# Output projections by token halves, with each half's norm and FFN operand blocks made apart

## The chip, the cores and the metric

The program runs on one core of one Trainium2 chip. The time is that of one execution on the device, in microseconds; the median of a few runs is given, and one more execution was profiled. In the profile PE is TensorE's matmuls, PEld its weight loads, DVE is VectorE, ACT ScalarE, POOL GpSimd, SP the sync engine that issues most DMAs. L12 is line 12 of the kernel.

## What is computed

A trunk of two layers over x of 1024 tokens by 1024 features, in float32. Layer 0 mixes tokens by sliding-window attention, layer 1 by "forgetting" attention; behind each follow the output projection with a residual, a norm, and a SwiGLU FFN with 2816 hidden features.

```python
for i in range(DEPTH):
    h = _rmsnorm(x, norm_mix[i])
    ...
        mix = _swa_sink_mixer(h, swa_w_in[j], swa_sinks[j], swa_w_out[j], cos, sin)
    ...
        mix = _fox_mixer(h, fox_w_in[j], fox_f_bias[j], fox_w_out[j])
    x = x + mix.astype(x.dtype)
    h = _rmsnorm(x, norm_ffn[i])
    x = x + _swiglu(h, ffn_w_gate_up[i], ffn_w_down[i]).astype(x.dtype)
return _rmsnorm(x, norm_final)
```

## The kernel before

**Form.** Everything is kept transposed: features on the 128 partitions, tokens along the row. x is `x_t`, 8 feature tiles (KD = 8) of 1024 tokens; "half" 0 and 1 are tokens 0 to 511 and 512 to 1023. A float32 product is made of three matmuls on parts: each operand has a high part (ScalarE, a copy into fp32r) and a low part (VectorE, raw minus high), and high x high, high x low and low x high are summed in PSUM. So each weight strip is loaded (SP), gets `w_hi` (ScalarE, `high`) and `w_lo` (VectorE, `low`), and is then used by TensorE. There are two buffers of each; semaphore `w_split` counts finished low parts, `mm_done` finished half strips, `evac_done` evacuated ones.

**Order.** Each engine's program is written out by hand, and the engines meet by semaphores. There is no scheduler; an engine does its own list in order, and a wait holds up all that stands behind it.

**Output projection** (`out_projection` on PE, `update_out` on ACT and DVE). A strip is 128 output features; strip m is done over half 0 and half 1 (24 matmuls of 512 tokens each) into bank 0 or 1, resp. 2 or 3. `out_first` does most of strip 0 while the attention is ending. VectorE adds each half strip to x (`add_strip`), ScalarE squares it and stores the strip of x to DRAM, GpSimd adds the squares up in `ssq`. While the last strips run, the first FFN weight tile is split (`weight_high`, `weight_low`).

**Head of the FFN** (`ffn`, `norm_sums`, `norm_bc`, `blocks_dve`, `block_high`). TensorE sums `ssq` over the partitions into bank 5 (L1703), ScalarE takes the root, VectorE makes the factor by six short steps and a diagonal (L1203 to L1214), TensorE spreads it over the partitions (L1710), ScalarE copies it to `rstd_ffn`. VectorE then makes normed blocks of x: `n00`, `n10` (half 0), `n01`, `n11` (half 1), 4 feature tiles each, and three more from their differences; seven blocks `b`, each with a high and a low part. The FFN's first product is done by Strassen's scheme in the form of Winograd: seven products (NP = 7, 12 matmuls each) per hidden tile instead of eight. There are 22 hidden tiles (FT) in a layer; tile r has gate and up weights `a_raw`, sums of these (`weight_sums` on GpSimd), and seven split blocks `a`. Products 4 to 6 wait for copies that ScalarE and VectorE take out of PSUM (`p1_keep`, `p5_keep`, `p57_keep`). The products of tile 0 and 1 stand one behind the other.

**Down projection.** The hidden tiles go through DRAM (`hid_scr`) and come back in three groups of 8, 6 and 8 tiles (`set_full`), are split into `set_hi` and `set_lo`, and every group is run over 8 strips. The first four tiles of group 0 come back early into `hid_pre`. TensorE begins groups 1 and 2 when all `set_lo` of the group are there.

**Entry of layer 1.** `update_ffn` adds the last strips; ScalarE makes `h_hi` from them, and VectorE makes the 16 half pieces of `h_lo` when all strips are done.

## Time and profile before

| | us |
|---|---|
| median of 3 runs | 2517.53 |
| lowest and highest run | 2513.55, 2517.95 |
| the profiled execution | 2513.21 |
| its span, from the first to the last instruction | 2511.1 |
| TensorE busy (share of the span) | 2340.7 (93%) |
| VectorE busy | 1369.9 (55%) |
| ScalarE busy | 971.9 (39%) |
| GpSimd busy | 592.3 (24%) |

The mean granted clock of TensorE was 0.967 of full speed. The page's slices show it below full speed at the start and at two places, about 450 to 500 us and 1750 to 1850 us from the start; there also the busy share of TensorE falls. In these places the output projection of a layer has ended and its FFN begins. Matmuls overlap in the records (one of 512 columns is shown with 390 ns and follows the one before by 227 ns at full clock), so their starts are to be read rather than their sums.

### The profile page before, as it was taken

The page shows a single profiled execution, that of the slowest core. Times are in us where ns is not written, and L with a number is a line of the kernel's source. Part 1 is how long each engine was busy: PE and PEld are TensorE (multiplying, and loading weights), DVE is VectorE, ACT ScalarE, POOL GpSimd, SP SyncE. Part 2 cuts the span into 40 slices and gives each one's busy share as a digit, 9 for nine tenths or more (in the row PEclk, how much of TensorE's full clock was granted, in tenths as well). Part 3 has the DMA queues.
Part 4 walks back from the last instruction along what each step waited for, and adds up shares of the span by engine and source line. Part 5 has one row for each costly group of instructions (what it writes and reads, how often), then busy time and mean ns, then how long its engine had stood idle before and what let it go on. Part 6 is the DMA issues. An engine that isn't in the chain of part 4 may idle for free.

```text
span 2511.1 us, 33488 instructions
## 1 busy us (share of the span) xinstructions
PE 2340.7 (93%) x11188; PEld 1931.9 (77%) x11188; DVE 1369.9 (55%) x2174; ACT 971.9 (39%) x1866; POOL 592.3 (24%) x423
## 2 busy tenths in 40 slices
PE   4998999699999999999999989989699999999998
PEld 3776777488888887786888778878478888888777
DVE  7797952844445443324633489982664444453422
ACT  3116942433333421232212289982343333331223
POOL 3232423133233100020000056652222322300011
PEclk6999999799999999999999999999799999999999
DMA  5258433022322262222444587745122222252311
GB/s 188 84 174 202 94 118 117 25 76 81 94 75 75 100 226 67 84 101 68 141 136 151 177 192 167 167 112 173 42 72 79 75 86 90 75 205 84 118 46 75
DMA packets 289811, 283.38 MB, mean 113 GB/s; under 512 B 64704, under 2 KB 253504, under 8 KB 285008
## 3 DMA queue, kind: packets, MB, share of 16 engines
q1 hardware_dynamic: 269536, 225.60, 31.7%
q10 hardware_dynamic: 20208, 56.92, 6.1%
q8 instruction: 37, 0.61, 0.1%
q14 instruction: 30, 0.25, 0.0%
HBM read 200.63 MB, written 81.85 MB: 112 GB/s over the span
## 4 chain that ended last, share of the span: by engine, by line
PE 78%; DVE 14%; ACT 3%; issue 2%; POOL 1%; ACTq 1%; DMA 0%; SPq 0%; DVEq 0%; POOLq 0%
PE psum L1688 12%; PE psum L1690 12%; PE psum L1689 12%; PE psum L1920 11%; PE psum L1922 11%; PE psum L1924 11%; PE psum L1814 2%; DVE work_b L1579 2%; PE psum L1832 2%; PE psum L1833 1%; DVE b_lo L1405 1%; PE psum L1781 1%; PE psum L1782 1%; DVE swa_p_lo L1297 1%; DVE neg_max L1261 1%
## 5 line engine op out<-in xcount | busy, mean ns | idle before, releaser
L1920 PE MATMUL psum<-b_hi,a_hi 128*128 128x512 f32 x1232 | 484.7, 393 | 38.6 <-DVE b_lo L1405 33.6
L1922 PE MATMUL psum<-b_lo,a_hi 128*128 128x512 f32 x1232 | 483.5, 392 | 0.0
L1924 PE MATMUL psum<-b_hi,a_lo 128*128 128x512 f32 x1232 | 483.2, 392 | 0.0
L1920 PEld LDWEIGHTS psum<-b_hi,a_hi 128*128 128x128 f32 x1232 | 233.9, 190 | 92.6 <-issue 38.0
L1688 PE MATMUL psum<-set_hi,dw_hi 128*128 128x512 f32 x704 | 277.2, 394 | 16.0 <-DVE set_lo L1443 16.0
L1360 DVE TENSOR_TENSOR x_t<-psum,x_t 128x512 f32<-128x512 f32 (+1 forms) x128 | 88.4, 692 | 371.8 <-PE psum L1690 357.0
L1689 PE MATMUL psum<-set_lo,dw_hi 128*128 128x512 f32 x704 | 276.6, 393 | 0.0
L1690 PE MATMUL psum<-set_hi,dw_lo 128*128 128x512 f32 x704 | 276.4, 393 | 0.0
L1924 PEld LDWEIGHTS psum<-b_hi,a_lo 128*128 128x128 f32 x1232 | 233.9, 190 | 49.1
L1922 PEld LDWEIGHTS psum<-b_lo,a_hi 128*128 128x128 f32 x1232 | 234.0, 190 | 48.6
L1688 PE MATMUL psum<-h_hi,w_hi 128*128 128x512 f32 x576 | 230.3, 400 | 19.6 <-DVE w_lo L1184 14.3
L693 POOL TENSOR_TENSOR score<-score,inv_l 128x128 f32<-128x128 f32 (+7 forms) x128 | 155.4, 1225 | 383.1 <-DVE inv_l L1278 383.0
L727 POOL TENSOR_TENSOR a_sum<-a_raw 128x512 f32<-128x512 f32 x88 | 116.0, 1319 | 487.9 <-DVE a_lo L1400 487.4
L1689 PE MATMUL psum<-h_lo,w_hi 128*128 128x512 f32 x576 | 227.4, 395 | 0.0
L1690 PE MATMUL psum<-h_hi,w_lo 128*128 128x512 f32 x576 | 227.1, 394 | 0.0
L1400 DVE TENSOR_TENSOR a_lo<-a_sum,a_hi 128x512 fp32r<-128x512 f32 x176 | 125.9, 718 | 102.4 <-ACT a_hi L976 102.1
L1688 PEld LDWEIGHTS psum<-set_hi,dw_hi 128*128 128x128 f32 x704 | 133.6, 190 | 47.3 <-issue 16.3
L976 ACT ACTIVATE a_hi<-a_sum 128x512 fp32r<-128x512 f32 x176 | 109.7, 628 | 132.3 <-PE psum L1924 132.3
L1689 PEld LDWEIGHTS psum<-set_lo,dw_hi 128*128 128x128 f32 x704 | 133.7, 190 | 28.1
L1690 PEld LDWEIGHTS psum<-set_hi,dw_lo 128*128 128x128 f32 x704 | 133.7, 190 | 27.8
L795 ACT ACTIVATE dw_hi<-dw_raw 128x1024 fp32r<-128x1024 f32 x48 | 50.7, 1055 | 255.1 <-PE psum L1690 255.1
L1688 PEld LDWEIGHTS psum<-h_hi,w_hi 128*128 128x128 f32 x576 | 110.4, 192 | 46.0 <-issue 16.2
(193 smaller groups left out, 4269.6 us busy)
## 6 DMA issues: line engine op xcount, KB each, us to landing
a_raw<-in_ffn_w_gate_up SPq DMA_DIRECT2D x88, 512.0 KB, 5.0
hid_scr<-hid_out SPq DMA_DIRECT2D x44, 512.0 KB, 5.8
set_full<-hid_scr SPq DMA_DIRECT2D x18, 1024.0 KB, 6.1
x_t<-x_scr SPq DMA_DIRECT2D x16, 1024.0 KB, 7.4
dw_raw<-in_ffn_w_down SPq DMA_DIRECT2D x32, 512.0 KB, 4.1
x_scr<-x_t ACTq DMA_DIRECT2D x24, 512.0 KB, 2.7
w_raw<-in_fox_w_in SPq DMA_DIRECT2D x24, 512.0 KB, 4.0
fox_qk_hi<-part_hi ACTq DMA_DIRECT2D x16, 512.0 KB, 2.6
```

Source lines behind the costliest of these rows:

```text
L693: last = nc.gpsimd.tensor_tensor(sc, sc, inv_l[sl][:, i:i + 1].to_broadcast([P, fox_w(t)]), ALU.mult)
L727: nc.gpsimd.tensor_tensor(a_sum[dst][:, :, :], in0, in1, op).then_inc(a_summed, 1)
L795: nc.scalar.activation(dw_hi[p][:, :, :], dw_raw[p][:, :, :], ACT.Copy).then_inc(w_high, 1)
L976: nc.scalar.activation(a_hi[i][:, :, :], a_block(q, i), ACT.Copy).then_inc(a_high, 1)
L1360: V.tensor_tensor(xs, bank[2 * p + h].unsqueeze(1), xs, ALU.add).then_inc(evac_done, 1)
L1400: V.tensor_tensor(a_lo[i][:, :, :], a_block(q, i), a_hi[i][:, :, :].bitcast(FP32), ALU.subtract)\
L1688: T.matmul(bank[2 * p + h], whi[:, k, :], mh[:, k, half(h)], start=k == 0, stop=False)
L1689: T.matmul(bank[2 * p + h], whi[:, k, :], ml[:, k, half(h)], start=False, stop=False)
L1690: last = T.matmul(bank[2 * p + h], wlo[:, k, :], mh[:, k, half(h)], start=False, stop=k == n - 1)
L1920: T.matmul(out_ps, a_hi[i][:, j, :], b_hi[i][:, j, :], start=not more and j == 0, stop=False, skip_group_check=True)
L1922: T.matmul(out_ps, a_hi[i][:, j, :], b_lo[i][:, j, :], start=False, stop=False, skip_group_check=True)
L1924: last = T.matmul(out_ps, a_lo[i][:, j, :], b_hi[i][:, j, :], start=False, stop=j == KH - 1, skip_group_check=True)
```

## The change

1. **The output projection goes by token halves.** It now has 16 steps j = 0 to 15 per layer: strips 0 to 7 over half 0, then strips 0 to 7 over half 1, each 24 matmuls into bank j mod 4. Every strip of weights is loaded and split for each half. `o_hi` and `o_lo` are two tiles each, one per half.
2. **Norm and blocks of half 0 are made during half 1.** After step 9 the sums of half 0 are taken, after step 10 the factor is spread, and `n00`, `n10` and the parts of blocks 0 and 1 are made in steps 11 to 14. The square of strip 7 isn't added up by GpSimd but summed by TensorE directly, so there are two short matmuls for each of four token tiles.
3. **The splits of the first FFN weight tile** are spread over steps 2 to 8; its loads and those of tile 1 come ahead of the strip loads of step 4 and later.
4. **Look-ahead products.** Product 0 of tile 0 comes before the sums of half 1, product 1 of tile 0 behind them, then the factor is spread, then come products 0 and 1 of tile 1, then 2 to 6 of each. `prod_mm` is split into `prod_a` (products 0, 1) and `prod_b`.
5. **Down projection.** `hid_pre` is gone. Group 0 is taken in the order 6, 7, 0 to 5, tiles 6 and 7 being loaded after product 1 of the last tile, the others after product 3. In groups 1 and 2 `set_hi` and `set_lo` stand ahead of the weight split and the addition of the same strip.
6. **Entry of layer 1.** The pieces of `h_lo` are made strip by strip, and the first two weight strips of layer 1 go into the buffers of the down projection.
7. **A new memory map.** Nearly all tiles have other addresses, and there is a third buffer for the keys in layer 0. Other than above, no order or wait changes in attention, input projections and the FFN loop.

The core of the diff:

```diff
+        K_ORDER = (6, 7, 0, 1, 2, 3, 4, 5)
...
+            def load_out(c0, view, layer):
+                for j in range(2, 4):
+                    load_out_w(c0, view, j)
+
+                sp.wait_ge(mm_done, 2 * (c0 + 1))
+                load_a(layer, 0, 0)
+                load_a(layer, 1, 1)
+                for j in range(4, 2 * KD):
+                    load_out_w(c0, view, j)
...
-                sp.dma_start(hid_pre[:, :, :], hid_scr[:, 0:4, :]).then_inc(pre_in, 16)
...
+                sp.wait_ge(prod_a, 2 * (last + 1))
...
+                load_set(0, 3, 0)
+                load_d(c0, 0, 0, n0)
+                sp.wait_ge(prod_b, 5 * last + 2)
+                load_set(0, 0, 0)
+                load_set(0, 1, 0)
+                load_set(0, 2, 0)
...
+                    act.wait_ge(*prod_at(r, 5))
+                    set0_high(layer, (2, 3, 4, 5))
...
                 for m in range(KD):
-                    d_high(c0 + m + 2, m % 2)
                     if m >= 2:
                         if m % 2 == 0:
-                            act.wait_ge(set_in[1 + m // 2], 16 * (2 * layer + 1))
+                            act.wait_ge(set_in[m // 2 - 1], 16 * (2 * layer + 1))
                         set_high_of(set_hi[1][:, m - 2, :], set_full[1][:, m - 2, :])
+                    d_high(c0 + m + 2, m % 2)
...
+            def update_out(c0, layer, back, k):
+                for j in range(2 * KD):
+                    h, m = j // KD, j % KD
+                    if j == 0:
+                        dve.wait_ge(x_back[back], 16)
+                    if j == 2:
+                        dve.wait_ge(x_back[back + 1], 48)
+                    dve.wait_ge(mm_done, 2 * (c0 + j) + 2)
+                    V.tensor_tensor(x_t[:, m, half(h)], bank[j % 4], x_t[:, m, half(h)], ALU.add).then_inc(evac_done, 2)
+                    if j < 2 * KD - 2:
+                        low(c0 + j + 2, j % 2)
+                    if 0 <= j - 2 < NP:
+                        weight_low(FT * layer, 0, j - 2)
+                    if j == KD + 2:
+                        norm_diag(k, 0)
+                    if j == KD + 3:
+                        dve.wait_ge(rstd_ready, 2 * k + 1)
+                        normed(layer, k, n00, 0, 0)
+                    if j == KD + 4:
+                        normed(layer, k, n10, 1, 0)
+                    if j == KD + 5:
+                        block_low(layer, 0, n00)
+                    if j == KD + 6:
+                        block_low(layer, 1, n10)
...
+            def out_projection(a, c0, k, layer):
+
+                pe.wait_ge(w_split, c0 + 2)
                 out_first(a, 1, range(early_tiles(a)), True)
 
                 pe.wait_ge(a.o_free, a.groups * a.units)
-                for h in range(2):
-                    out_first(a, h, range(early_tiles(a), KD), False).then_inc(mm_done, 1)
-                chunk(c0 + 1, 1, KD, o_hi, o_lo)
-                linear_rest(c0, KD // 2, KD, o_hi, o_lo)
...
+                for m in range(2):
+                    out_first(a, m, range(early_tiles(a), KD), False).then_inc(mm_done, 2)
+                for j in range(2, 2 * KD):
+                    h, p = j // KD, j % 2
+                    pe.wait_ge(w_split, c0 + j + 1)
+                    if j >= 4:
+                        pe.wait_ge(evac_done, 2 * (c0 + j - 3))
...
+                    last.then_inc(mm_done, 2)
+                    if j == KD + 1:
+                        norm_sums(k, 0)
+                    if j == KD + 2:
+                        norm_bc(k, 0)
...
             def ffn(layer, c0, k):
-                norm_sums(k)
-                norm_bc(k)
-                r0 = FT * layer
-                products(r0, 0, NP * layer)
-                products(r0 + 1, 1)
+                r0, b0 = FT * layer, NP * layer
+                pe.wait_ge(evac_done, 2 * (c0 - 1))
+                product(r0, 0, 0, b0)
+                norm_sums(k, 1)
+                product(r0, 0, 1, b0)
+                norm_bc(k, 1)
+                for i in range(2):
+                    product(r0 + 1, 1, i)
+                for i in range(2, NP):
+                    product(r0, 0, i, b0)
+                for i in range(2, NP):
+                    product(r0 + 1, 1, i)
```

**The order at three places.** A row is an instruction with output, inputs and what it waits for; a number behind a name tells buffers apart, and x2 is a repeat. First, PE where the early part of the output projection of layer 0 ends, before and after:

```order
L1848 MATMUL psum<-o_hi_93,w_hi0_121 128x512
L1849 MATMUL psum<-o_lo_94,w_hi0_121 128x512
L1850 MATMUL psum<-o_hi_93,w_lo0_123 128x512
L1688 MATMUL psum<-o_hi_93,w_hi1_122 128x512 [waits evac_done,w_split]
```

```order
L1905 MATMUL psum<-o_hi0_95,w_hi1_126 128x512
L1906 MATMUL psum<-o_lo0_97,w_hi1_126 128x512
L1907 MATMUL psum<-o_hi0_95,w_lo1_128 128x512
L1964 MATMUL psum<-o_hi0_95,w_hi0_125 128x512 [waits w_split]
```

Before, the second strip (buffer 1) follows on the first; now both have been done for half 0, and the third strip, in buffer 0 again, follows.

Second, DVE in layer 0 from the projection's end to the first normed block before, and around the factor of half 0 (step 10) after:

```order
L1360 TENSOR_TENSOR x_t_49<-psum,x_t_49 128x512 [waits mm_done] x2
L1203 TENSOR_SCALAR nat_v_212<-psum 128x8 [waits sd_done]
...
L1214 TENSOR_TENSOR diag_ffn_166<-ident_204,nat_y_213 128x1024 [waits newton]
L1414 SCALAR_TENSOR_TENSOR n00_189<-x_t_49,gains_209,rstd_ffn_167 128x512 [waits rstd_ready]
L1414 SCALAR_TENSOR_TENSOR n00_189<-x_t_49,gains_209,rstd_ffn_167 128x512 x3
```

```order
L1415 TENSOR_TENSOR x_t_49<-psum,x_t_49 128x512 [waits mm_done]
L1226 TENSOR_TENSOR w_lo0_127<-w_raw0_123,w_hi0_125 128x1024 [waits w_high]
L1247 TENSOR_SCALAR nat_v_217<-psum 128x4 [waits sd_done]
...
L1259 TENSOR_TENSOR diag_ffn_173<-ident_209,nat_y_218 128x512 [waits newton]
L1415 TENSOR_TENSOR x_t_49<-psum,x_t_49 128x512 [waits mm_done]
L1226 TENSOR_TENSOR w_lo1_128<-w_raw1_124,w_hi1_126 128x1024 [waits w_high]
L1463 SCALAR_TENSOR_TENSOR n00_194<-x_t_49,gains_214,rstd_ffn_174 128x512 [waits rstd_ready]
L1463 SCALAR_TENSOR_TENSOR n00_194<-x_t_49,gains_214,rstd_ffn_174 128x512 x3
```

The factor now stands behind the addition and the weight split of step 10, and the first normed block behind those of step 11.

Third, DVE at the last strip of group 1 of the down projection (`dw_lo` is the low part of a weight strip), before and after:

```order
L1360 TENSOR_TENSOR x_t_49<-psum,x_t_49 128x512 [waits mm_done] x2
L1190 TENSOR_TENSOR dw_lo1_197<-dw_raw1_193,dw_hi1_195 128x1024 [waits w_high]
L1443 TENSOR_TENSOR set_lo0_200<-set_full0_202,set_hi0_198 128x1024 [waits set_high]
```

```order
L1491 TENSOR_TENSOR set_lo0_205<-set_full0_207,set_hi0_203 128x1024 [waits set_high]
L1405 TENSOR_TENSOR x_t_49<-psum,x_t_49 128x512 [waits mm_done] x2
L1232 TENSOR_TENSOR dw_lo1_202<-dw_raw1_198,dw_hi1_200 128x1024 [waits w_high]
```

The set's low part stood last in the strip and now stands first.

## Rows read from the trace of the kernel before

**Rows 1.** Waits of PE over the span: us in total, times, longest.
```profile
PE psum L1920 <- DVE b_lo L1405: 33.6, 4, 8.6
PE psum L1688 <- DVE set_lo L1443: 16.0, 8, 3.7
PE psum L1688 <- DVE h_lo L1392: 5.3, 1, 5.3
```

**Rows 2.** Timeline of PE, head of layer 0: start, us, instruction, [idle before <-releaser].
```profile
435.62 3.09 PE L1703 MATMUL psum<-ones,ssq 128*128 128x1 f32 x16 [2.87 <-POOL ssq L747]
...
442.55 3.78 PE L1710 MATMUL psum<-diag_ffn,ones 128*128 128x512 f32 x4 [3.85 <-DVE diag_ffn L1214]
454.74 0.76 PE L1920 MATMUL psum<-b_hi,a_hi 128*128 128x512 f32 x1 [8.40 <-DVE b_lo L1405]
...
471.17 0.76 PE L1920 MATMUL psum<-b_hi,a_hi 128*128 128x512 f32 x1 [8.22 <-DVE b_lo L1405]
...
484.53 0.47 PE L1920 MATMUL psum<-b_hi,a_hi 128*128 128x512 f32 x1 [2.13 <-ACT p_keep L1014]
```

**Rows 3.** Stretches: us; busy PE, PEld, DVE, ACT, POOL; PEclk, DMA share, GB/s.
```profile
432.60:509.10 76.50, 51.03 (x189) 39.50 (x189) 58.06 (x60) 30.82 (x36) 16.86 (x13) 0.80 0.10 32
1778.50:1857.00 78.50, 52.00 (x189) 40.15 (x189) 58.03 (x60) 30.92 (x36) 16.85 (x13) 0.76 0.10 31
471.20:476.70 5.50, 5.50 (x13) 4.33 (x14) 5.50 (x3) 4.41 (x3) 0.00 (x0) 0.50 0.00 0
982.00:986.00 4.00, 3.97 (x11) 3.13 (x12) 0.00 (x0) 0.00 (x0) 0.00 (x0) 0.57 1.10 346
1147.10:1153.10 6.00, 5.99 (x14) 4.72 (x15) 6.00 (x10) 0.00 (x0) 0.00 (x0) 0.51 0.32 87
```

**Rows 4.** Timeline of DVE, steady projection of layer 0.
```profile
389.38 0.69 DVE L1360 TENSOR_TENSOR x_t<-psum,x_t 128x512 f32 x1 [4.73 <-PE psum L1690]
391.93 1.42 DVE L1184 TENSOR_TENSOR w_lo<-w_raw,w_hi 128x1024 fp32r<-128x1024 f32 x1 [1.86 <-ACT w_hi L789]
394.82 0.69 DVE L1360 TENSOR_TENSOR x_t<-psum,x_t 128x512 f32 x1 [1.47 <-PE psum L1690]
```

**Rows 5.** Timeline of PE, first matmul of group 1, down projection of layer 0.
```profile
982.03 0.52 PE L1688 MATMUL psum<-set_hi,dw_hi 128*128 128x512 f32 x1 [3.69 <-DVE set_lo L1443]
```

**Rows 6.** Timeline of DVE, the last set_lo before it.
```profile
980.67 1.22 DVE L1443 TENSOR_TENSOR set_lo<-set_full,set_hi 128x1024 fp32r<-128x1024 f32 x1
```

**Rows 7.** Timeline of DVE, head of layer 0: diagonal, two normed blocks, low part of block 0.
```profile
441.27 1.23 DVE L1214 TENSOR_TENSOR diag_ffn<-ident,nat_y 128x1024 f32<-128x1024 f32 x1
447.00 5.39 DVE L1414 SCALAR_TENSOR_TENSOR n<-x_t,gains,rstd_ffn 128x512 f32<-128x512 f32 x8 [4.50 <-ACT rstd_ffn L807]
452.31 2.28 DVE L1405 TENSOR_TENSOR b_lo<-n,b_hi 128x2048 fp32r<-128x2048 f32 x1
```

**Rows 8.** Timeline of DVE, last weight split before layer 1's first matmul.
```profile
1144.86 1.45 DVE L1184 TENSOR_TENSOR w_lo<-w_raw,w_hi 128x1024 fp32r<-128x1024 f32 x1 [2.31 <-ACT w_hi L789]
```

**Rows 9.** A stretch at the end of the FFN products of layer 0, as rows 3.
```profile
884.00:890.00 6.00, 6.00 (x28) 4.95 (x28) 3.76 (x6) 3.40 (x5) 0.00 (x0) 1.00 1.01 390
```

**Rows 10.** Timeline of PE, first matmul of the second strip, layer 0.
```profile
356.43 0.39 PE L1688 MATMUL psum<-o_hi,w_hi 128*128 128x512 f32 x1
```

**Rows 11.** Timeline of ACT, high part of the third strip, layer 0.
```profile
361.90 1.06 ACT L789 ACTIVATE w_hi<-w_raw 128x1024 fp32r<-128x1024 f32 x1 [3.85 <-DMA w_raw<-in_swa_w_out]
```

**Rows 12.** Timeline of DVE, low part of the third strip, layer 0.
```profile
362.99 1.23 DVE L1184 TENSOR_TENSOR w_lo<-w_raw,w_hi 128x1024 fp32r<-128x1024 f32 x1 [5.67 <-ACT w_hi L789]
```

**Rows 13.** Timeline of ACT, head of layer 0: three high parts of blocks in a row.
```profile
468.86 5.51 ACT L990 ACTIVATE b_hi<-b_full 128x2048 fp32r<-128x2048 f32 x3 [5.26 <-DVE b_full L1420]
```

**Rows 14.** DMA issues: KB each, median us from issue to landing.
```profile
w_raw<-in_swa_w_out SPq DMA_DIRECT2D x8, 512.0 KB, 5.1
```

**Rows 15.** Timeline of POOL in the same stretch.
```profile
390.97 1.29 POOL L747 TENSOR_TENSOR ssq<-ssq,sq 128x512 f32<-128x512 f32 x1 [4.07 <-ACT sq L924]
```

**Rows 16.** Tile set_full, 850 to 960 us.
```profile
DMA to landing us min/median/max: 5.1/6.2/11.3
```

More of the change, by code:

```diff
@@ L992, in set_high_of, with set0_high, products_act @@
             def set_high_of(dst, src):
                 nc.scalar.activation(dst, src, ACT.Copy).then_inc(set_high, 1)
-            def products_act(r, q, last=False, layer=0, c0=0):
+            def set0_high(layer, ks):
+                for k in ks:
+                    if k % 2 == 0:
+                        act.wait_ge(set0_in[k // 2], 16 * (layer + 1))
+                    set_high_of(set_hi[0][:, k, :], set_full[0][:, k, :])
+            def products_act(r, q, first=False, last=False, layer=0, c0=0):
@@ L997, in products_act @@
                 bk = lambda i: prod_bank(q, i)
-                act.wait_ge(prod_mm, NP * r + 1)
+                act.wait_ge(*prod_at(r, 0))
                 wait(act, c_done, 4 * r - 3)
                 nc.scalar.activation(p1_keep[:, :], bk(0), ACT.Copy).then_inc(p1_kept, 1)
-                if not last:
+                if not last and not first:
                     weight_high(r + 1, 1 - q, 0)
                     weight_high(r + 1, 1 - q, 1)
-                else:
-                    act.wait_ge(pre_in, 16 * (layer + 1))
-                    for k in range(4):
-                        set_high_of(set_hi[0][:, k, :], hid_pre[:, k, :])
@@ L1443, in set_low_of, with set0_low, products_dve @@
                 V.tensor_tensor(dst, src, high_part.bitcast(FP32), ALU.subtract).then_inc(set_low, 1)
-            def products_dve(r, j, q, last=False, layer=0, c0=0):
+            def set0_low(layer, at0, ks):
+                for n, k in enumerate(ks):
+                    dve.wait_ge(set_high, FT * layer + at0 + n + 1)
+                    set_low_of(set_lo[0][:, k, :], set_full[0][:, k, :], set_hi[0][:, k, :])
+            def products_dve(r, j, q, first=False, last=False, layer=0, c0=0):
                 bk = lambda i: prod_bank(q, i)
@@ L1490, in products_dve @@
                 if last:
-                    for k in range(4, 6):
-                        dve.wait_ge(set_high, FT * layer + k + 1)
-                        set_low_of(set_lo[0][:, k, :], set_full[0][:, k, :], set_hi[0][:, k, :])
-                dve.wait_ge(prod_mm, NP * r + 7)
+                    set0_low(layer, 4, (2, 3, 4, 5))
+                dve.wait_ge(*prod_at(r, 6))
                 V.tensor_tensor(hid_h[0], bk(6), u2_keep[:, :], ALU.add).then_inc(c_done, 1)
@@ L1675, in _, with chunk @@
             T = nc.tensor
-            def chunk(c, p, n, mh, ml, ready=None, after=None, w=(w_hi, w_lo)):
+            def chunk(c, p, n, mh, ml, ready=None, after=None, w=(w_hi, w_lo), order=None):
                 whi, wlo = w[0][p], w[1][p]
@@ new lines, in product @@
+            def product(r, q, i, blocks=None):
+                pe.wait_ge(a_low, NP * r + i + 1)
+                if blocks is not None:
+                    pe.wait_ge(b_low, blocks + i + 1)
+                if i == 4:
+                    pe.wait_ge(p1_kept, r + 1)
+                if i == 5:
+                    pe.wait_ge(p5_kept, r + 1)
+                if i == 6:
+                    pe.wait_ge(p57_kept, r + 1)
+                out_ps, more = prod_bank(q, i), i >= 4
+                for j in range(KH):
+                    T.matmul(out_ps, a_hi[i][:, j, :], b_hi[i][:, j, :], start=not more and j == 0, stop=False,
+                             skip_group_check=True)
+                    T.matmul(out_ps, a_hi[i][:, j, :], b_lo[i][:, j, :], start=False, stop=False,
+                             skip_group_check=True)
+                    last = T.matmul(out_ps, a_lo[i][:, j, :], b_hi[i][:, j, :], start=False, stop=j == KH - 1,
+                                    skip_group_check=True)
+                last.then_inc(prod_at(r, i)[0], 1)
@@ L1986, in _ @@
             attention(fox)
[L1987 removed]
+            out_projection(fox, C_O1, 3, 1)
             ffn(1, C_F1, 3)
```

598 lines of the change are left out of this document (292 added, 306 removed).

## The prediction

> **What bounds the kernel now.** I read the waits of TensorE first, then its timeline around the longest of them, then the other engines' timelines at those places. TensorE is busy nearly throughout, so its waits are the time to be won. Three belong to what the change touches: on b_lo, the low parts of the activation blocks (33.6 us, four waits), on set_lo (16.0 us, eight waits) and on h_lo (5.3 us, one) [rows 1]. The b_lo waits stand in one place in each layer, which I call the head: from the last matmul of the output projection to the end of the first two tiles of FFN products. In layer 0 TensorE waits there 2.87, 3.85, 8.40, 8.22 and 2.13 us, and has 3.09 us of column sums and 3.78 us of spreading matmuls between [rows 2]. The head takes 76.5 us in layer 0 and 78.5 in layer 1, at a granted clock of 0.80 and 0.76 [rows 3]. VectorE adds into x one half strip of 24 matmuls every 5.44 us in the steady projection (389.38 to 394.82) [rows 4], so a product of 12 takes 2.72 us and the 14 products of the head 38.1. The heads therefore lose 38.4 and 40.4 us, **78.8 us** together; with the set and h waits that is all the change can touch.
>
> **Price of a low clock.** After the 8.22 us wait the granted clock is 0.50 for 5.5 us: 2.7 us lost. After a 3.69 us wait it is 0.57 for 4 us: 1.7 us; the other three of this kind I read the same way, a little less, 6.1 us for all four. After the h_lo wait it is 0.51 for 6 us: 2.9 us [rows 3].
>
> **Part 1, group changes of the down projection: a gain of 20.9 us.** Four times TensorE waits 3.69 us at the start of a group, for the last set_lo, which VectorE does behind the last strip's addition and the next weight split [rows 5, 6]. The change puts set_hi and set_lo ahead of these, so the last set_lo is made while the last strip (8.2 or 10.9 us of matmuls) still runs: its set_hi comes behind the weight split of two strips ahead, about 2.2 us into that strip, and set_lo is done by 3.5 us. VectorE's addition now stands behind set_lo; who waits for it is the bank's next use, a whole strip later. 4 x 3.69 + 6.1 = 20.9. What then is late is nothing on TensorE.
>
> **Part 2, into layer 1: a gain of 6.5 us.** The 16 h_lo pieces (0.67 us each, the rate of [rows 7]) are made strip by strip, and only those of the last two strips are left at the end. From the end of the last strip: addition 0.8, h_hi and square 1.2, weight high part 1.05, weight low part 1.45 [rows 8], two pieces 1.35 and one 0.67, that is 6.5 us, where TensorE reaches the last piece after 21 matmuls, 4.8 us. A wait of 1.7 us stands for 5.3 + 2.9.
>
> **Part 3, end of the FFN products: a loss of 3.8 us.** The early 2 MB load of hid tiles 0 to 3 is gone. Instead tiles 6 and 7 come after the second product of the last tile and 3 MB after the fourth. DMA moved 390 GB/s in the like stretch of before [rows 9], so 3 MB are in about 9.5 us after issue, while 8.2 us of products remain. That alone would be covered, since the tiles come one by one. But set_hi of tiles 2 to 5 now writes over a block that product six reads. After that product come an addition (0.7) that stands behind two set_lo, a Silu (0.6), then set_hi and four set_lo at 1.2 us. By my schedule the last is ready 7.2 us after the last product, TensorE wants it after 4.8 (21 matmuls): 2.5 us lost. Before lost (16.0 - 14.8) / 2 = 0.6. So 1.9 more in each layer.
>
> **Part 4, the head and the projection before it: a loss of 8.0 us.** The same matmuls, but what TensorE loses changes place. I list what it loses in a layer, in order.
> (a) Third strip. TensorE used to do strip 2 over both halves (10.9 us) after the early strip; strip 2 is now done for one half, ahead. It arrives where it used to start strip 2, at 356.43 [rows 10], and needs strip 3, whose raw weights land behind 4 MB of x: high part at 361.90, low part from 362.99 for 1.23 us [rows 11, 12]. The order of the loads hasn't changed. Wait 7.8 us, clock 2.7.
> (b) The sums for the first half: 3.1, eight pairs of short matmuls as before, now twice in a layer.
> (c) Spreading of the first half. TensorE reaches it right after strip 11 of 16; VectorE starts the factor only behind the addition and weight split of that same strip. Addition to end of split 3.95 us (389.38 to 391.93, plus 1.42) [rows 4], factor and half a diagonal 2.1 (the row's 1.23 us is a whole one [rows 7]; the step in which GpSimd isn't in the way is short). Wait 6.0, matmul 1.0, clock 2.7: 9.7.
> (d) Strips 12 to 16. VectorE has per half strip 3.95 us of chain in 5.44; with four normalising instructions more (2.7; eight take 5.39 [rows 7]) it has 6.7 us and falls behind by 1.3 and 2.6 us, then has a block's low part (2.28) too. Only strip 16 comes late, by 0.9.
> (e) Second sums 3.1. The square they need is ready under the first look-ahead product.
> (f) Second spreading: from the sums' end to it 3.84 us before [rows 2], less half a diagonal 0.6, under a product of 2.72: wait 0.5, matmul 1.0.
> (g) Block 3 (n01, a difference, n11, its low part): copy 0.7 + 2.7 + 2.2 + 2.7 + 2.3 = 10.6 us, under two look-ahead products, 5.4: wait 5.2, clock 2.7.
> (h) Block 4: two differences and a low part, 6.6 us against a product with low clock, 5.4: wait 1.4 with the signal.
> (i) Block 5. ScalarE's last three high parts took 5.51 us in a row [rows 13], 1.84 each; two of them now wait for the last difference, and p1_keep comes behind: 2.2 + 3.7 + 0.6 against 2.7: wait 3.8, clock 1.5. p5_keep then is just in time.
> Sum 10.5 + 3.1 + 9.7 + 0.9 + 3.1 + 1.5 + 7.9 + 1.4 + 5.3 = 43.4 us a layer, 86.8 for both against 78.8. The work of VectorE that went under the projection (two blocks, seven splits of a) is real, about 14 us a layer; (a), (c) and the second sums take it back.
>
> **Supply.** Each strip is loaded and split twice, 0.5 MB every 5.44 us in place of 10.9. A load is issued when the split of two strips before is done and has 8.3 us; it took 5.1 [rows 14]. Two 1 MB loads of a go ahead of strip 5 now; the 7.8 us wait covers them. GpSimd does its four a_sum ahead of the squares' sums, also under that wait. At nothing, then; bounds 0 and the rival below.
>
> The split took 1.42 us with a GpSimd addition (1.29) beside it, 1.23 without [rows 4, 12, 15]: 0.2 us, under cover in my sum. The Trainium skill (SBUF — State Buffer, "SBUF: two separate sides") says that such a VectorE instruction and GpSimd's take a shared port pair as a lock, and the loser waits for the whole of the other. By it strips 13 to 15, where VectorE is behind already, could each lose up to 1.29 us, and (d) would grow by some 2 us: 2506 in place of 2502. The row, of an instruction that came late into the addition, doesn't contradict it.
>
> **Sum.** -20.9 - 6.5 + 3.8 + 8.0 = -15.6 us. The profiled execution took 2513.2 (span 2511.1), so 2497.6; it lies 4.3 under the median of the three runs, 2517.5, against which I forecast **2502**.
>
> **Rivals.** First, *the heads gain after all*: strip 3 lands 1 us earlier, as no x store runs beside it, the short steps of the factors take no contention (1.5 in all) and the clock costs half (4.8). That is 7.3 us a layer: 2487. For it, the clock fell back for one stretch only after 3.69 us; against it, (a), (c) and (g) are over 5 us each, like the waits that cost 2.7.
> Second, *no change*: VectorE is the bound of the whole second half. It misses each strip from 13 on and the differences slip; some 7 us a layer more, 2516. For it, (d) has no slack at all; against it, chain (c) is measured with its neighbours.
> Third, *slower, by weight supply*: if a strip's load takes L us, each of six pairs of strips in two layers waits L - 8.3. The loads of 1 MB landed in 5.1 to 11.3 us [rows 16]; at 11.3 it is 12 x 3.0 = 36, 2538. It decides from 10.1 us on (12 x 1.8 = 21). Against it, 5.1 us with half the traffic.
>
> **How the numbers follow.** The forecast, 2494 to 2510, has 0.52, the gaining heads 0.17, no change 0.19, slower 0.12. For 8 in 10 the range goes from 2485, half of the first rival, to 2518, where the second ends. 0.2% is 5 us, about what a measurement can tell: faster is below 2512.5, all of the first two and a quarter of the third, 0.74; same 0.14; slower 0.12.
>
> **What the profile after would show.** Right: no wait on set_lo of 3.7 us; a wait of about 8 us for w_lo at the third strip of both projections and of 6 before the first spreading matmul; the b_lo waits down from 33.6 to about 14; a wait near 2 us at the entry of layer 1. Wrong: a wait for a weight split at every strip (third rival), or third strip and first spreading without a wait, when the sum would be 25 us or more better.

## The result and the profile after

| | before | after |
|---|---|---|
| median of 4 runs each, on one chip, us | 2516.30 | 2490.56 |
| lowest and highest | 2513.55, 2517.95 | 2488.18, 2493.86 |
| span of the profiled execution, us | 2511.1 | 2490.1 |
| mean granted clock of it | 0.967 | 0.976 |

The ratio is 0.9903 (95% interval 0.9891 to 0.9914): **faster by 25.7 us**, 21.0 between the two profiled executions. The forecast was 2502 us, 15.6 below.

Those waits of TensorE in the kernel after that answer to [rows 1] or are new (us in total, times, longest):

```profile
PE psum L1986 <- DVE b_lo L1457: 20.1, 6, 5.4
...
PE psum L1964 <- DVE w_lo L1226: 14.4, 5, 7.9
PE psum L1768 <- DVE diag_ffn L1259: 11.5, 2, 5.8
...
PE psum L1738 <- DVE set_lo L1491: 3.1, 8, 1.1
...
PE psum L1738 <- DVE h_lo L1437: 1.5, 2, 1.2
```

The wait on set_lo fell from 16.0 to 3.1 us and the one on h_lo from 5.3 to 1.5. The waits on b_lo fell from 33.6 to 20.1, but the line on w_lo, of the output projection, is new, and the line on diag_ffn grew from 7.6 (3.85 of it in [rows 2]) to 11.5. So in the output projection and the head the waits changed place more than they went away. For b_lo the forecast was about 14: the 7.0 us above it are twice the wait of 3.50 us, which the prediction had given to a copy, and run 7 shows that the copy ended it.

TensorE's timeline of the same kernel through layer 0, in order of time, answers to [rows 2, 5, 10]:

```profile
365.63 0.79 PE L1964 MATMUL psum<-o_hi,w_hi 128*128 128x512 f32 x1 [7.88 <-DVE w_lo L1226]
...
424.85 1.22 PE L1768 MATMUL psum<-diag_ffn,ones 128*128 128x512 f32 x1 [5.75 <-DVE diag_ffn L1259]
...
451.09 0.50 PE L1964 MATMUL psum<-o_hi,w_hi 128*128 128x512 f32 x1 [0.39 <-DVE w_lo L1226]
...
476.10 0.77 PE L1986 MATMUL psum<-b_hi,a_hi 128*128 128x512 f32 x1 [5.38 <-DVE b_lo L1457]
...
482.71 0.47 PE L1986 MATMUL psum<-b_hi,a_hi 128*128 128x512 f32 x1 [1.15 <-DVE b_lo L1457]
...
489.20 0.76 PE L1986 MATMUL psum<-b_hi,a_hi 128*128 128x512 f32 x1 [3.50 <-DVE b_lo L1457]
...
897.28 0.50 PE L1738 MATMUL psum<-set_hi,dw_hi 128*128 128x512 f32 x1 [0.98 <-DVE set_lo L1491]
...
983.10 0.39 PE L1738 MATMUL psum<-set_hi,dw_hi 128*128 128x512 f32 x1
```

The first six are items (a), (c), (d), (g), (h), (i) of the prediction's fourth part. The last is the first matmul of group 1: where [rows 5] shows a wait of 3.69 us there is none.

To see where 21.0 us went I cut both spans at the same matmuls (columns: us between the two cuts):

| stretch | before | after | change |
|---|---|---|---|
| attention, up to where TensorE turns to the second (after: third) strip | 356.43 | 357.75 | +1.3 |
| layer 0: rest of projection and head, to the end of the first two tiles' products | 152.71 | 154.87 | +2.2 |
| end of the FFN products to group 1's first matmul | 92.09 | 89.68 | -2.4 |
| group 1, group 2 | 159.63 | 152.33 | -7.3 |
| entry of layer 1 and fox attention | 560.68 | 557.29 | -3.4 |
| layer 1: projection and head | 154.69 | 153.22 | -1.5 |
| layer 1: as lines 3 and 4 | | | -9.6 |
| end | 21.54 | 21.24 | -0.3 |

The FFN loops between the cuts take 380.80 us in both. The two down projections are the only large item.

### The profile page after: what moved, and what is told of

Its sections match the earlier page's. It is cut to its first block, busy times and chain, and to the rows that moved or that the text cites. A ratio compares the mean times of both kernels' runs of the same rounds, so it can differ in the third digit from the quotient of the medians.

```text
span 2490.1 us, 33386 instructions
## 1 busy us (share of the span) xinstructions
PE 2339.4 (94%) x11220; PEld 1930.0 (78%) x11220; DVE 1398.7 (56%) x2204; ACT 987.2 (40%) x1884; POOL 589.5 (24%) x419
## 4 chain that ended last, share of the span: by engine, by line
PE 77%; DVE 14%; ACT 4%; issue 2%; DMA 2%; POOL 1%; ACTq 1%; SPq 0%; DVEq 0%
PE psum L1986 11%; PE psum L1988 11%; PE psum L1990 11%; PE psum L1738 10%; PE psum L1739 10%; PE psum L1740 10%; PE psum L1872 2%; DVE work_b L1629 2%; PE psum L1964 2%; PE psum L1890 2%; PE psum L1965 2%; PE psum L1966 2%; PE psum L1891 1%; PE psum L1839 1%; PE psum L1840 1%
## 5 line engine op out<-in xcount | busy, mean ns | idle before, releaser
L1986 PE MATMUL psum<-b_hi,a_hi 128*128 128x512 f32 x1232 | 484.8, 393 | 20.1 <-DVE b_lo L1457 20.1
L1738 PE MATMUL psum<-h_hi,w_hi 128*128 128x512 f32 x544 | 216.1, 397 | 14.5 <-DVE w_lo L1226 14.5
L1740 PE MATMUL psum<-h_hi,w_lo 128*128 128x512 f32 x544 | 213.7, 393 | 0.0
L1739 PE MATMUL psum<-h_lo,w_hi 128*128 128x512 f32 x544 | 213.7, 393 | 0.0
L1405 DVE TENSOR_TENSOR x_t<-psum,x_t 128x512 f32<-128x512 f32 x96 | 66.1, 690 | 237.1 <-PE psum L1740 226.3
L824 ACT ACTIVATE w_hi<-w_raw 128x1024 fp32r<-128x1024 f32 x66 | 69.3, 1050 | 170.5 <-PE psum L1740 162.8
```

Of the source, the lines that this page charges most:

```text
L824: nc.scalar.activation(w_hi[p][:, :, :], w_raw[p][:, :, :], ACT.Copy).then_inc(w_high, 1)
L1405: V.tensor_tensor(xs, bank[2 * p + h].unsqueeze(1), xs, ALU.add).then_inc(evac_done, 1)
L1738: T.matmul(bank[2 * p + h], whi[:, k, :], mh[:, k, half(h)], start=i == 0, stop=False)
L1739: T.matmul(bank[2 * p + h], whi[:, k, :], ml[:, k, half(h)], start=False, stop=False)
L1740: last = T.matmul(bank[2 * p + h], wlo[:, k, :], mh[:, k, half(h)], start=False, stop=i == n - 1)
L1986: T.matmul(out_ps, a_hi[i][:, j, :], b_hi[i][:, j, :], start=not more and j == 0, stop=False, skip_group_check=True)
```

## Experiments

Times are medians. The kernels of this section ran in three groups, each on one chip beside runs of the kernel before: 1 to 3 and 5 (before 2516.0 us), 4, 6, 7 and the first of 8 (2514.2), the rest (2515.8). The kernel before thus differs by up to 2 us between groups; where that matters, the ratio to it is used as well. The traces are cut as in the table above, and "head" means the rest of the projection and the head. Numbers of runs below are those of the headings.

### 1 and 2. The group order alone, and everything but it

The edit of the first, in the kernel before; the second is its reverse in the kernel after.

```diff
                     for m in range(KD):
-                        add_strip(c0 + KD * gi + m, m, m % 2)
-                        d_low(c0 + KD * gi + m + 2, m % 2)
...
                             set_low_of(set_lo[1 - gi][at0], set_full[1 - gi][at0], set_hi[1 - gi][at0])
+                        add_strip(c0 + KD * gi + m, m, m % 2)
+                        d_low(c0 + KD * gi + m + 2, m % 2)
```

ScalarE's `d_high` goes behind `set_high_of` in the same way.

> The kernel before, with one part of the change alone: in each output group of the FFN's down projection the products of a set stand ahead of the ones whose operand pieces are made late, in the order of the kernel after. Nothing else differs. Theory (the group order brings nearly all of the gain): minus 20 to 24 us, so about 2494 us; in the trace the two groups of a layer lose the waits on set_lo that they had (group 1 of layer 0 ends about 5.5 us sooner after its start, its start about 4 us sooner), and the heads are as before. Rival (the output projection by halves and the block entry bring the gain, the groups only fill other waits): minus 0 to 8 us, about 2512 us.

> The kernel after with that one part undone: the groups in the order of the kernel before, all else as after. Theory: plus 20 to 24 us over the kernel after, so about 2513 us, close to the kernel before, because the rest of the change nets only minus 2 to minus 4 us (the entry of layer 1 minus 4.7, the heads plus 0.7, the end of the FFN's products has its price of 3.0 from h_lo). Rival: the rest of the change holds its own gain of 10 us or more, and this kernel stays under 2505 us.

Measured: 2490.6 us for the groups alone, 25.3 below the kernel before and a little more than the 20 to 24 expected (ratio to before 0.9902, 0.9887 to 0.9917), 2511.5 for the rest alone (0.9984, 0.9974 to 0.9993). The wait on set_lo in the groups-alone kernel, and VectorE's last set_lo of group 1, which stood right ahead of the waiting matmul in [rows 6]:

```profile
PE psum L1688 <- DVE set_lo L1443: 1.2, 4, 0.5
```

```profile
970.43 1.23 DVE L1190 TENSOR_TENSOR dw_lo<-dw_raw,dw_hi 128x1024 fp32r<-128x1024 f32 x1 [0.46 <-ACT dw_hi L795]
971.58 1.22 DVE L1443 TENSOR_TENSOR set_lo<-set_full,set_hi 128x1024 fp32r<-128x1024 f32 x1
974.72 0.69 DVE L1360 TENSOR_TENSOR x_t<-psum,x_t 128x512 f32<-128x512 f32 x1 [1.93 <-PE psum L1690]
```

It ends at 972.8; group 1 begins at 979.96. The addition, now behind it, waits for TensorE and not the other way round. From the first matmul of group 0 to the last of group 2 it is 240.34 us where before took 251.5, in each layer: 22.3 us in all. **The group order brings all of the gain, and the other three parts together bring nothing beside it that these runs can tell from none.** With the old groups they gained 4.5 us, a little more than the 2 to 4 us expected of them, so the pair was run once more on one chip.

> The kernel before with the group order alone, once more, beside the kernel after on one chip, to tell whether the rest of the change (output projection by halves, h_lo with the strips, memory map) moves the time at all where the groups are in order. By the landmarks of the two first traces the rest costs 1.3 us; by the run of the kernel after with the old groups it gains 4.5 us; by the single run of the groups alone it is nothing. Theory: within 2 us of the kernel after. Rival (the rest gains, as in the run with the old groups): 3 to 6 us above the kernel after.

> The kernel after as it is, on the same chip as the groups alone. Theory: 2490 us, within 2 us of the groups alone. Rival: 3 to 6 us below them.

Measured: 2491.3 and 2489.8 us, 1.5 apart, as the theory had it and in either's spread (2489.7 to 2492.7 and 2487.8 to 2491.1). Cut by cut between these two traces, the rest of the change costs 3.7 us up to the end of layer 0's head and 1.5 at the end of the FFN's products of each layer, and gets 8.3 back from the end of layer 0's down projection to the end of layer 1's head.

### 3. The third strip's weight

```diff
             def load_out(c0, view, layer):
-                for j in range(2, 4):
-                    load_out_w(c0, view, j)
...
                 k = 2 if a.fox else 0
+                for j in range(2, 4):
+                    load_out_w(C_O1 if a.fox else C_O0, w_out_view["fox" if a.fox else "swa"], j)
                 sp.wait_ge(a.pv_done, a.groups * a.units - 1)
```

> The kernel after; the loads of strips 2 and 3 of the output weight are issued on SyncE's queue ahead of the load of x, whose issue waits for the attention products to be done. Theory (the third strip's products wait for their weight because its load is queued behind that issue): the wait of 7.9 us on w_lo in layer 0 falls to about 2.7 us and that of 5.6 us in layer 1 to about 3.3 us, and with the lower clock behind them gone the kernel gains 8 to 11 us, about 2481 us. Rival (VectorE's own work, the splits and the sums of squares that stand ahead, sets the wait): the wait stays above 6 us and 4.5 us and the time moves by less than 2 us.

Measured: 2484.6 us (0.9880, 0.9865 to 0.9895), 6 us below the kernel after: less than expected. In layer 1 the third strip's wait went from 5.55 to 3.07 and the head took 148.7 us in place of 153.2. In layer 0 TensorE now has two waits. The first is at the third strip, the second two strips later, at strip 4 counted from 0, the fifth; the expectations call it the fourth:

```profile
358.41 0.50 PE L1963 MATMUL psum<-o_hi,w_hi 128*128 128x512 f32 x1 [2.39 <-DVE w_lo L1225]
...
375.06 0.50 PE L1963 MATMUL psum<-o_hi,w_hi 128*128 128x512 f32 x1 [3.84 <-DVE w_lo L1225]
```

Following w_lo back, over ScalarE to GpSimd, in the same kernel:

```profile
371.20 0.63 ACT L970 ACTIVATE sq_ffn<-x_t 128x512 f32<-128x512 f32 x1 [10.63 <-POOL ssq_ffn L767]
371.73 1.04 ACT L823 ACTIVATE w_hi<-w_raw 128x1024 fp32r<-128x1024 f32 x1
```

```profile
365.16 2.66 POOL L749 TENSOR_TENSOR a_sum<-a_raw 128x512 f32<-128x512 f32 x2 [24.68 <-DMA a_raw<-in_ffn_w_gate_up]
```

ScalarE stood 10.63 us at a square whose buffer GpSimd had not read, and GpSimd stood behind its a_sum, which wait for a_raw.

### 4. That chain, and ScalarE's order

On top of 3 (`sum_squares_out` now calls `weight_sums` itself, behind its step 1; the same in layer 1):

```diff
-            weight_sums(0, 0)
-            sum_squares_out(0)
+            sum_squares_out(0, 0)
...
                     h, m = j // KD, j % KD
+                    if j < 2:
+                        high(c0 + j + 2, j % 2)
                     act.wait_ge(evac_done, 2 * (c0 + j) + 2)
```

> The kernel with early loads of strips 2 and 3 (it gained only 5.9 us, since a new wait of 3.84 us stood at the fourth strip of layer 0), and two orders more: GpSimd makes the a_sum pieces, which wait for a_raw, behind its second sum of squares and not ahead of the first; ScalarE makes w_hi of strips 2 and 3 ahead of the squares of x of strips 0 and 1. Theory (the fourth strip waited on w_lo, that on w_hi, that on a square that waited for GpSimd, and GpSimd stood in order behind the load of a_raw): the 3.84 us go to under 0.5, the third strip's wait falls from 2.4 and 3.1 us to under 1.5 us, and the kernel comes to 2474 to 2479 us. Rival (the fourth strip's weight is late by its load): 3 us or more stay at the fourth strip of layer 0, and the time stays above 2481 us.

Measured: 2478.7 us (0.9864, 0.9849 to 0.9880), 6 us below run 3, within the theory's number. But at strip 4 of layer 0 (the expectation's fourth) **the rival was right**: 4.35 us of wait are there still, and now it is the load:

```profile
371.50 0.50 PE L1965 MATMUL psum<-o_hi,w_hi 128*128 128x512 f32 x1 [4.35 <-DVE w_lo L1227]
```

```profile
368.86 1.06 ACT L823 ACTIVATE w_hi<-w_raw 128x1024 fp32r<-128x1024 f32 x1 [5.65 <-DMA w_raw<-in_swa_w_out]
```

That strip's load is issued behind four a_raw loads of 0.5 MB. GpSimd was only the later of two causes. The third strips now wait 1.11 and 1.79 us (under 1.5 was expected of both), and the two heads are 3.0 and 3.2 us shorter than in run 3.

### 5. The first half's spreading, one step later

```diff
-                    if j == KD + 2:
+                    if j == KD + 3:
                         norm_bc(k, 0)
```

and the same for ScalarE's copy of it.

> The kernel after; the spreading of the first half's norm over the partitions (the products of diag_ffn with ones, and the copy of them) is moved one step later in the loop of the second half, behind the next strip's products. Theory (TensorE stands in order behind a product whose operand VectorE makes late, while the next strip's products are ready): the waits of 5.75 us on diag_ffn, which cost 9.9 and 9.0 us with their clock, shrink to under 1.5 us each, and the kernel gains 14 to 18 us, about 2475 us. Rival (the next strip's weight is no sooner there than diag_ffn, or the first look-ahead products then wait for the copy): the wait moves to w_lo or to b_hi and b_lo, and the gain is under 5 us.

Measured: 2473.4 us (0.9837, 0.9824 to 0.9850), 17.1 below the kernel after; the two heads are 8.0 and 8.3 us shorter. TensorE's timeline at the spreading:

```profile
423.66 0.70 PE L1768 MATMUL psum<-diag_ffn,ones 128*128 128x512 f32 x1 [0.34 <-DVE diag_ffn L1259]
```

The clock, by stretches of 4 us behind that place (columns as in [rows 3]), first of the kernel after, then of this one:

```profile
424.80:428.80 4.00, 3.95 (x7) 2.49 (x8) 0.00 (x0) 0.60 (x1) 0.00 (x0) 0.50 0.31 93
```

```profile
423.60:427.60 4.00, 3.94 (x15) 2.93 (x16) 2.35 (x3) 2.06 (x3) 1.30 (x1) 1.00 0.68 237
```

5.75 us of wait gave 0.50 (the lower level, 1.2 GHz) behind it, 0.34 us gave 1.00. So item (c), 9.9 us in the kernel after and 9.7 in the prediction, was nearly all wait and low clock (the spreading itself stays), and it is a matter of one step in TensorE's order: the product was asked for one strip before VectorE could have made its operand.

### 6. h_lo at the end again

```diff
-                    if c_next and m:
-                        low_part(m - 1)
                 if c_next:
-                    low_part(KD - 1)
+                    for m in range(KD):
+                        low_part(m)
```

> The kernel after, with one part undone: VectorE makes all eight pieces of h_lo after the last strip of layer 0's FFN, as in the kernel before, instead of one with each strip. Theory (this part brings the gain of layer 1's entry, 4.7 us between the two traces): TensorE's wait on h_lo goes from 1.2 back to about 5.3 us, with a low clock behind it, and the kernel is 4 to 7 us slower than the kernel after, about 2496 us. Rival (the pieces beside the strips cost VectorE as much on the strips as they save at the end): within 1.5 us of the kernel after.

Measured: 2494.4 us (0.9925, 0.9911 to 0.9938), above the kernel after by 3.8 us of medians or, with each beside its own kernel before, by 5.5; the theory had 4 to 7. The wait is 5.30 us again, and from the end of group 2 to TensorE's second strip of layer 1 it takes 17.0 us where the kernel after took 9.4. So the part is worth some 4 to 8 us, which the output projection, the heads and the end of the products give back.

### 7. The copy to p1_keep

```diff
                 norm_spread(k, 1)
+                keep_first(r0, 0)
                 for i in range(2, NP):
                     block_high(layer, i)
```

> The kernel after; ScalarE copies product 0's bank to p1_keep (for block 0 of the first FFN strip pair) before it makes b_hi of blocks 2 to 6, not behind all five. The wait in question is the third one in the FFN's first products, 3.50 us in each layer, which the trace puts down to VectorE's b_lo; product 4 also waits for that copy, which in the kernel after starts at 488.48, behind two b_hi of 3.71 us. Theory (the copy, not b_lo, ends the wait): the wait falls to 1.2 to 1.6 us, and with its clock the kernel gains 4 to 7 us over the two layers, about 2485 us. Rival (b_lo of block 4 ends it, as the trace says): the wait stays at 3.5 us and the time within 1.5 us of the kernel after.

(`keep_first` is the copy to p1_keep. Product 4, counted from 0, is the prediction's block 5.) Measured: 2491.1 us (0.9911, 0.9897 to 0.9924): no change, although the wait behaved as in the theory. TensorE at products 4 and 5:

```profile
484.84 0.47 PE L1991 MATMUL psum<-b_hi,a_hi 128*128 128x512 f32 x1 [1.35 <-issue]
...
491.03 0.47 PE L1991 MATMUL psum<-b_hi,a_hi 128*128 128x512 f32 x1 [3.21 <-ACT p_keep L1055]
```

The theory was right on what ended the 3.50 us: with only the copy moved, it fell to 1.35, although the trace named b_lo. And the gain was nil, since product 5 waits for the next copy, p5_keep. On ScalarE that stands behind the same b_hi and a Silu, and the Silu itself waits 2.13 us for an addition that VectorE makes behind all its low parts. The prediction had called p5_keep "just in time"; it was so only because block 5 was late.

### 8. All of them, and the waits that came next

> All of the orders together: the kernel after with the first half's norm spread one step later, early loads of strips 2 and 3, the two orders of GpSimd and ScalarE, and the early copy to p1_keep. Theory (the waits are apart in time, so their prices add): minus 17 (late spread) minus 14 (loads and orders) minus 5 (copy) from 2490.6, so 2450 to 2459 us. Rival (each wait that goes uncovers the next, most of all that of the first products on b_lo, 5.4 us, whose operands VectorE makes no sooner): less than two thirds of that sum, above 2466 us.

Measured: 2463.8 us (0.9804, 0.9791 to 0.9818), between theory and rival. The parts had by themselves -17.1, -11.9 and +0.5, together -28.5; measured -26.8. So they add; what was too high were the sizes expected of the loads with their orders (14, measured 11.9) and of the copy (5, measured nothing).

> The kernel with all orders (2463.8 us), and three steps more, each against the wait that came in the place of one taken away: ScalarE also copies product 2's bank to p5_keep ahead of b_hi of blocks 5 and 6 (the wait on p_keep of 3.2 us in each layer), VectorE makes p57_keep ahead of the first a_lo piece there, and the load of strip 4's weight is issued ahead of the second a_raw (the wait of 2.1 us at the fourth strip of layer 0). Theory (each of these waits stands behind a step that is only in the wrong place in its engine's order): both waits on p_keep fall under 1 us and the fourth strip's under 0.5 us, 8 to 11 us with their clock, so 2453 to 2456 us. Rival (VectorE is the limit there, whatever the order): the waits move to b_lo or p57_keep of block 6 at over 2 us in each layer, and the time stays above 2460 us.

```diff
+                load_out_w(c0, view, 4)
                 load_a(layer, 1, 1)
...
                 for i in range(2, NP):
+                    if i == 5:
+                        keep_third(r0, 0)
                     block_high(layer, i)
```

(`keep_third` is the copy to p5_keep), and VectorE's p57_keep one a_lo piece sooner. Measured: **2450.1 us (0.9744, 0.9731 to 0.9757)**, 13.7 below the one before it by medians. The forecast was 2453 to 2456, a gain of 8 to 11. By the profiled spans it is 7.4 (2459.6 and 2452.2), the one before being its fastest execution and this one its slowest; the two heads are 5.8 and 3.1 us shorter, 8.9 in all. So the theory's size fits, and no trace shows where the rest of the 13.7 lies. TensorE at strip 4, at blocks 3, 4 and 5, and at the next tile's block 6 (product 5 counted from 0):

```profile
369.21 0.50 PE L1979 MATMUL psum<-o_hi,w_hi 128*128 128x512 f32 x1 [0.80 <-DVE w_lo L1239]
...
457.20 0.77 PE L2001 MATMUL psum<-b_hi,a_hi 128*128 128x512 f32 x1 [5.39 <-DVE b_lo L1470]
...
463.80 0.47 PE L2001 MATMUL psum<-b_hi,a_hi 128*128 128x512 f32 x1 [1.36 <-DVE b_lo L1470]
468.16 0.47 PE L2001 MATMUL psum<-b_hi,a_hi 128*128 128x512 f32 x1 [1.38 <-issue]
...
486.39 0.47 PE L2001 MATMUL psum<-b_hi,a_hi 128*128 128x512 f32 x1 [1.46 <-ACT p_keep L1046]
```

The waits went less far than forecast. Strip 4's went from 2.13 to 0.80 us, not under 0.5. The first tile no longer waits for p5_keep in either layer, but the next tile now does, for 1.46 and 1.41 us.

This kernel beats both: 65.7 us below the kernel before, measured beside it, and some 40 below the one after, with the same matmuls. What stays of the head is block 3's 5.39 us in each layer, which is VectorE's chain of four pieces n01, a difference, four pieces n11 and a low part; that was not attacked.

## Why the prediction came out as it did

The sign held, and so did the mechanism of each part: the group order pays, and the rest, forecast at +5.3 us, comes to about nothing. The median of 2490.6 lies in the wide range (2485 to 2518) but below the narrow one (2494 to 2510). By the cuts of the profiled pair, forecast -15.6, measured -21.0. The medians are 25.7 apart; the other 4.7 us are no term of the sum but the place of the two profiled executions among the others of their kernels, which spread over 4.4 and 5.7 us.

**Part 1, groups.** Forecast -20.9, measured -22.3 (table above and run 1). The waits of 3.69 us are gone, and the clock behind them was worth a little more than read.

**Part 2, entry.** Forecast -6.5, measured -4.7. The wait came out right (forecast 1.7; 1.16 and 0.36 us). The 2.9 us of low clock were taken as gone altogether. In this trace they were not: the stretch of the kernel after behind the two waits, columns as in [rows 3],

```profile
1142.70:1151.60 8.90, 8.90 (x42) 7.57 (x41) 2.33 (x8) 0.27 (x1) 0.00 (x0) 0.81 0.44 117
```

has a clock of 0.81, where 7 matmuls follow each other by 0.43 us, not 0.23, right behind the 16 short ones of the norm's sums. That gives 1.4 back. But it is one execution's number: in the second trace of the same kernel (the last of runs 1 and 2), behind the same two waits and the same short matmuls, the clock stayed at 1.00. Of the nine traces with this entry three show the low clock and six do not.

**Part 3, end of the products.** Forecast +3.8, measured +3.0. TensorE waits four times on set_lo, 0.98 us (1.10 in layer 1) and three times 0.17, which with the slower first matmul behind each wait costs 2.6 us, where I had 2.5. But what the kernel before lost there was 1.2 us in a layer, not 0.6.

**Part 4, heads.** Forecast +8.0, measured +0.7. This is the term that was off. Loss of TensorE in a layer, us, by item:

| item | forecast | layer 0 | layer 1 |
|---|---|---|---|
| (a) third strip | 10.5 | 10.4 | 8.5 |
| (b) first sums | 3.1 | 1.85 | 1.85 |
| (c) first spreading | 9.7 | 9.9 | 9.0 |
| (d) strip 16 | 0.9 | 0.7 | 0.7 |
| (e) second sums | 3.1 | 1.85 | 1.7 |
| (f) second spreading | 1.5 | 1.1 | 1.1 |
| (g), (h), (i) blocks 3 to 5 | 14.6 | 14.8 | 15.1 |
| sum of items | 43.4 | 40.6 | 37.9 |

(Against the ideal 114.24 us of that stretch the losses are 40.6 and 39.0; 1.1 us of layer 1 has no item.) **The mis-sized step is (b) and (e)**: I took the 3.09 us of [rows 2] for 16 short matmuls over as they stood. But those ran behind a wait of 2.87 us, at a low clock. The stretch of before, and that of after:

```profile
435.60:438.70 3.10, 3.08 (x16) 3.00 (x16) 0.00 (x0) 0.00 (x0) 2.81 (x3) 0.59 0.05 20
```

```profile
411.60:413.50 1.90, 1.90 (x18) 1.86 (x18) 0.69 (x1) 0.00 (x0) 0.00 (x0) 1.00 0.85 239
```

At 0.59 they take 3.09 us, at 1.00 they take 1.85. In layer 1 of the kernel before they took 3.57 us at 0.50, and in all ten traces of the kernel after and its variants 1.84 at 1.00. The four places, two in each layer, make 5.0 of the 7.3 us between forecast and measured. Another 2.0 is (a) in layer 1: one value was taken for both layers, from layer 0's row, and in layer 1 the weight is there 2.3 us sooner. The three waits over 5 us, (a), (c), (g), and the copy behind (i) came out within 0.4 us in layer 0.

How far the whole term is settled is another matter. Both heads together take 307.4, 309.0 and 306.9 us in the three traces that have the heads of the kernel before (it and the groups alone, twice), and 308.1, 306.2, 305.9 and 303.3 in four that have those of the kernel after (it, twice, and the kernels of the second run and of run 6). So +0.7 is one pair's number. The heads did not become 8.0 us dearer, as forecast, and may have gained a little.

**Rest.** Forecast 0, measured +2.3 (1.3 us in the first attention, as much in fox attention). A difference of this size between two single traces needs no cause in the change. The second trace of the kernel after is 4.1 us shorter in span, and 4.4 of that lie from the end of layer 0's down projection to the end of layer 1's head. The clock accounts for most of it: the entry of layer 1 ran at 1.00 in place of the 0.81 above, worth about 1.5 us, and so did the stretch behind block 5's wait in layer 1, where the head is 1.8 us shorter. That wait was the same in both, 3.50 and 3.49 us (first the kernel after, then its second trace):

```profile
1821.40:1825.40 4.00, 3.99 (x10) 3.17 (x11) 2.79 (x2) 2.35 (x4) 0.00 (x0) 0.50 0.01 2
```

```profile
1818.40:1822.40 4.00, 2.95 (x12) 2.13 (x12) 2.76 (x2) 2.35 (x4) 0.00 (x0) 1.00 0.01 2
```

**The first rival, that the heads gain after all,** gave its chance to three things: an earlier strip 3 (so in layer 1 only), cheaper short steps (no), half the clock's price (no: 0.50 for 4 us behind (a) and (c)). Its time, 2487, is nearer to the median than mine, but that is luck: what made the heads cheaper than forecast were the sums, which it does not name, and 4.7 us of the median are no term at all. **No change** did not come: VectorE kept up from step 13 on; the only strip that waited for it was strip 16, 0.39 us. **Weight supply** did not decide either: the strip loads landed in 4.1 and 4.0 us (medians of 16), though runs 3 and 4 showed one late strip in layer 0.

**The port lock.** The prediction weighed the Trainium skill (SBUF — State Buffer, "SBUF: two separate sides") against a row that showed only 0.2 us. The kernel after has a plainer one, VectorE's split and what GpSimd did beside it:

```profile
376.56 2.24 DVE L1226 TENSOR_TENSOR w_lo<-w_raw,w_hi 128x1024 fp32r<-128x1024 f32 x1 [2.53 <-ACT w_hi L824]
```

```profile
375.00 2.72 POOL L770 TENSOR_TENSOR ssq_ffn<-ssq_ffn,sq_ffn 128x512 f32<-128x512 f32 x2
```

Alone the split takes 1.23 us [rows 12]; here it takes 1.0 more, close to the rest of GpSimd's second addition, which ends 1.2 us after it began. The whole trace bears this out. 32 splits of 128x1024 began while a GpSimd instruction was running; 0.36 to 1.18 us of that were left, and each split took 1.08 us more than what was left (1.44 to 2.26 us). The other 128 took 1.21 to 1.23 us, and 12 of these had begun first, with GpSimd's instruction coming after. Then it is GpSimd that takes longer: its a_sum took 2.23 us in place of 1.29 where it began 0.13 us after a split.

```profile
367.82 1.23 DVE L1226 TENSOR_TENSOR w_lo<-w_raw,w_hi 128x1024 fp32r<-128x1024 f32 x1 [1.65 <-ACT w_hi L824]
```

```profile
367.95 2.23 POOL L750 TENSOR_TENSOR a_sum<-a_raw 128x512 f32<-128x512 f32 x1 [27.34 <-DMA a_raw<-in_ffn_w_gate_up]
```

This agrees with that section. Its effect on item (d), which I had put at up to 2 us, was none: the last three splits began 0.38 us before an addition's end and lost 0.24 us each, not up to 1.29, and (d) came out at 0.7.

## What to carry to other kernels

An engine does its list in order, so look at each waiting instruction for what stands ready behind it. Here moving a few steps within the lists took 25 us (sets ahead of the addition) and 40 more (spreading, loads, copies), while the rest of the change, the restructured projection with it, brought nothing that could be told beside the group order. When a wait is removed, name what is late next before counting the gain: p5_keep took all that p1_keep had given.

A duration taken from the trace carries the clock of its place. Put the granted clock beside every row that becomes a term of a sum, above all for short matmuls behind a wait. And before a microsecond or two between two single traces gets a cause, look at the same stretch in a second trace of the same kernel.

## What the runs showed of the hardware

- In the 4 us behind a wait of TensorE the clock depends on more than the wait's length. In all traces of this case, from 150 to 2440 us, each of the 88 waits of 4.5 us or more was followed by 0.50 to 0.66, and of the 166 waits of 1.0 to 1.7 us all but one by 0.99 or more. Between them both occur. The wait of 3.48 to 3.51 us before block 5 stands in seven traces, in both layers: seven times it was followed by 1.00 and seven times by 0.50 to 0.60, in the two traces of the same kernel too. So its price is one or the other, and these runs do not show what decides.
- In the entry of layer 1 the low clock, where it came, came later than the waits of 1.16 and 0.36 us, behind the 16 short matmuls.
- A VectorE split and a GpSimd instruction that overlap do not share: whichever began second took longer, by nearly all that was left of the other (32 splits, and the a_sum above).
- The trace names as releaser of a wait for several semaphores the last by its records, and that can be the wrong engine: 3.50 us "on b_lo" were ended by ScalarE's copy, as run 7 showed by moving the copy alone.
